# Eight-bank input transposes, the residual's affine step on VectorE, and a later table product in a one-core hybrid mLSTM / sparse-attention / MoE layer

## What is computed

```python
h = concat([meta_tokens, x])                # (528, 1024)
h = layer_norm(h, ln_in_g, ln_in_b)         # input norm: also the residual
p = h @ w_in                                # all projections
...                                         # mLSTM branch, sparse attention branch
ckv = rms_norm(c_kv, kv_norm_g)
logits += rel_bias[bucket(distance)]        # table of 32 buckets x 8 heads
h = layer_norm(ALPHA * h + y @ w_out, ...)  # the residual h is used here
h = layer_norm(ALPHA * h + moe(h), ...)     # 16 experts, two of them per token
```

## Time and profile before

| | us |
|---|---|
| median of 3 runs | 841.85 |
| lowest, highest | 839.75, 842.48 |
| the profiled execution's own time | 842.93 |
| its span in the trace | 840.8 |
| TensorE busy in the span | 747.8 (89%) |
| VectorE busy | 590.2 (70%) |
| ScalarE busy | 428.3 (51%) |
| GpSimd busy | 103.1 (12%) |

### The profile page before, as it was taken

How to read it: one execution, slowest core, us unless ns; L and a number is a source line. 1 busy time by engine, 2 the same in 40 slices (tenths; PEclk the granted TensorE clock), 3 DMA queues, 4 the chain that set the end, 5 groups by cost and what they waited for, 6 DMA issues and landing times.

```text
span 840.8 us, 10786 instructions
## 1 busy us (share of the span) xinstructions
PE 747.8 (89%) x3980; PEld 604.7 (72%) x3982; DVE 590.2 (70%) x794; ACT 428.3 (51%) x498; POOL 103.1 (12%) x118
## 2 busy tenths in 40 slices
PE   3399999999899999999999859999999999999920
PEld 1296799897467677787888756788888888888710
DVE  4906999796236544443565778898988989988828
ACT  4433333434642544481222133778778787878712
POOL 4540000000001000000000202111112121112012
PEclk9999999999999899999999958999999999999975
DMA  8645231320050111143238863999999999995243
GB/s 198 201 127 195 85 99 53 101 87 14 0 202 3 50 52 51 51 178 123 101 95 317 323 225 104 358 397 385 397 398 400 396 396 391 398 395 215 64 191 131
DMA packets 102540, 167.09 MB, mean 199 GB/s; under 512 B 18848, under 2 KB 39584, under 8 KB 102504
## 3 DMA queue, kind: packets, MB, share of 16 engines
q1 hardware_dynamic: 95024, 145.53, 48.8%
q0 software_dynamic: 4752, 13.11, 4.0%
q10 hardware_dynamic: 2728, 7.95, 2.4%
HBM read 156.07 MB, written 17.42 MB: 206 GB/s over the span
## 4 chain that ended last, share of the span: by engine, by line
PE 81%; DVE 9%; ACT 3%; issue 3%; DMA 2%; SPq 1%; POOL 0%; POOLq 0%; DVEq 0%; ACTq 0%
PE low L1032 15%; PE low L1033 15%; PE low L1034 15%; PE wide L1032 7%; PE wide L1034 7%; PE wide L1033 7%; PE wide L1407 2%; PE low L1202 1%; PE low L1302 1%; PE wide L1187 1%; PE low L1264 1%; PE low L1359 1%; PE wide L1235 1%; SPq L397 1%; PE wide L1420 1%
## 5 line engine op out<-in xcount | busy, mean ns | idle before, releaser
L1791 DVE TENSOR_TENSOR m_lo<-m_raw,m_hi 128x2048 fp32r<-128x2048 f32 x95 | 214.9, 2289 | 28.8 <-ACT m_hi L911 28.1
L911 ACT ACTIVATE m_hi<-m_raw 128x2048 fp32r<-128x2048 f32 x95 | 179.8, 1918 | 23.8 <-PE low L1034 23.5
L1032 PE MATMUL low<-m_hi,xe_hi 128*128 128x512 f32 x256 | 103.0, 402 | 2.7 <-DVE xe_lo L1856 1.8
L1032 PE MATMUL low<-hT_hi,w_hi 128*128 128x512 f32 (+1 forms) x240 | 95.7, 399 | 10.6 <-issue 10.6
L1034 PE MATMUL low<-m_hi,xe_lo 128*128 128x512 f32 x256 | 100.0, 391 | 0.0
L1033 PE MATMUL low<-m_lo,xe_hi 128*128 128x512 f32 x256 | 99.7, 389 | 0.0
L1509 DVE TENSOR_TENSOR w_lo<-raw,w_hi 128x2048 fp32r<-128x2048 f32 x28 | 64.1, 2290 | 45.7 <-ACT w_hi L654 45.5
L1033 PE MATMUL low<-hT_lo,w_hi 128*128 128x512 f32 (+1 forms) x240 | 93.7, 390 | 0.0
L1034 PE MATMUL low<-hT_hi,w_lo 128*128 128x512 f32 (+1 forms) x240 | 93.0, 388 | 0.0
L654 ACT ACTIVATE w_hi<-raw 128x2048 fp32r<-128x2048 f32 x28 | 53.5, 1909 | 18.1 <-PE wide L1034 8.3
L1032 PEld LDWEIGHTS low<-hT_hi,w_hi 128*128 128x128 f32 x240 | 47.2, 197 | 20.4 <-issue 11.1
(11 more groups left out here) (348 smaller groups left out, 1438.4 us busy)
## 6 DMA issues: line engine op xcount, KB each, us to landing
m_raw<-in_w_gate SPq DMA_DIRECT2D x32, 1024.0 KB, 8.2
m_raw<-in_w_up SPq DMA_DIRECT2D x32, 1024.0 KB, 8.0
m_raw<-in_w_down SPq DMA_DIRECT2D x31, 1024.0 KB, 9.2
raw<-in_w_in SPq DMA_DIRECT2D x19, 1024.0 KB, 5.1
raw<-in_w_out SPq DMA_DIRECT2D x4, 1024.0 KB, 5.0
table_dram<-table_row ACTq DMA_DIRECT2D x1, 2624.0 KB
strips<-table_dram SPq DMA_DIRECT2D x8, 264.0 KB, 4.1
xn<-in_x SPq DMA_DIRECT2D x4, 512.0 KB, 5.6
```

The costliest lines, as they stand in the source:

```text
L911: nc.scalar.activation(m_hi[n % MS][:, :], (m_spare if is_last(n, j) else m_raw[slot])[:, :], ACT.Copy).then_inc(q["m_hi_ready"], 1)
L1032: nc.tensor.matmul(outp, lh, rh, start=first, stop=False)
L1791: v.tensor_tensor(m_lo[n % MS][:, :], (m_spare if is_last(n, j) else m_raw[n % MR])[:, :], m_hi[n % MS][:, :].bitcast(F32), ALU.subtract). ...
```

## The change

Five edits, all at the start of the program:

1. Each row tile's eight transposes are made as soon as the tile is normalised, into eight banks (block c into bank (4 + c) mod 8). The second pass of transposes with its wait on `lo_x` is gone. The meta transposes go to bank 4 and wait for `lo_x` at 1.
2. The residual's scale and bias move from GpSimd to VectorE, behind `w_lo` of unit 1.
3. ScalarE makes `w_hi` of unit 0 after block 1 of `hT_hi` and no longer before block 0.
4. The table product moves on TensorE from the front to just before the transposes L1119. `ftab` and its store move on ScalarE behind the second `qidxT`. Their two loads go behind `gbc` and `bbc`, which go ahead of the other late loads.
5. The squares go to `score` in place of `md`, so ScalarE's wait on `h_stored` moves down to the store of `table_dram`. GpSimd makes the two triangular masks between the powers of tiles 0, 1 and 2.

```diff
 @block.sync
-            sp.dma_start(relb[:, :], a["rel_bias"]).then_inc(q["table_in"], 16)
-            sp.dma_start(oneh[:, :], onehot).then_inc(q["table_in"], 16)
...
             load(1)
+            sp.dma_start(gbc[:, :], bcast_rows(a["ln_in_g"], D)).then_inc(q["load_late"], 16)
+            sp.dma_start(bbc[:, :], bcast_rows(a["ln_in_b"], D)).then_inc(q["load_late"], 16)
+            sp.dma_start(relb[:, :], a["rel_bias"]).then_inc(q["table_in"], 16)
+            sp.dma_start(oneh[:, :], onehot).then_inc(q["table_in"], 16)
             for i in range(CONV):
...
-            sp.dma_start(gbc[:, :], bcast_rows(a["ln_in_g"], D)).then_inc(q["load_late"], 16)
-            sp.dma_start(bbc[:, :], bcast_rows(a["ln_in_b"], D)).then_inc(q["load_late"], 16)
 @block.gpsimd
...
                 pool.wait_ge(q["rstd_ready"], i + 1)
+                if i == 0:
+                    step(nc.gpsimd.memset(tri_qs[:, :], 0.0))
...
+                elif i == 1:
+                    step(nc.gpsimd.memset(tri_st[:, :], 0.0))
...
-            pool.wait_ge(q["load_late"], 16 * 10)
-            pool.wait_ge(q["xt_done"], KC)
-            for i in range(TT):
-                pool.wait_ge(q["xn_ready"], i + 1)
-                step(nc.gpsimd.tensor_tensor(xn[:, i, :], xn[:, i, :], gbc[:, :], ALU.mult))
-                nc.gpsimd.tensor_tensor(xn[:, i, :], xn[:, i, :], bbc[:, :], ALU.add).then_inc(q["h_ready"], 1)
-                pool.wait_ge(q["h_ready"], i + 1)
 @block.scalar
-            act.wait_ge(q["table_done"], 1)
-            nc.scalar.activation(ftab[:, :], wide[0][0:AH, 0:FX], ACT.Copy).then_inc(q["table_out"], 1)
-            act.wait_ge(q["table_out"], 1)
-            act.dma_start(table_row, ftab[:, :]).then_inc(q["table_put"], 16)
...
-            split_hi(0)
             act.wait_ge(q["load_consts"], 16 * 2)
             for c in range(KC):
+                if c == 2:
+                    split_hi(0)
                 act.wait_ge(q["xt_done"], c + 1)
...
-            act.wait_ge(q["h_stored"], 16 * TT)
             for i in range(TT + 1):
...
-                square = nc.scalar.activation(md[0:n, 0:R], src, ACT.Square, accum_out=css[0:n, i:i + 1])
+                square = nc.scalar.activation(score[0:n, 0:R], src, ACT.Square, accum_out=css[0:n, i:i + 1])
...
-            act.wait_ge(q["h_stored"], 16 * TT)
             evac(B_QI, qidxT[:, 0, :])
             evac(B_QI + 1, qidxT[:, 1, :])
+            act.wait_ge(q["table_done"], 1)
+            nc.scalar.activation(ftab[:, :], wide[0][0:AH, 0:FX], ACT.Copy).then_inc(q["table_out"], 1)
+            act.wait_ge(q["table_out"], 1)
+            act.dma_start(table_row, ftab[:, :]).then_inc(q["table_put"], 16)
             split_hi(3)
+            act.wait_ge(q["h_stored"], 16 * TT)
 @block.tensor
...
-                for c in range(4):
-                    mm = nc.tensor.transpose(bank[4 + c][:, i * P:(i + 1) * P], xn[:, i, c * P:(c + 1) * P], ident[:, :])
+                for c in range(KC):
+                    mm = nc.tensor.transpose(bank[(4 + c) % 8][:, i * P:(i + 1) * P], xn[:, i, c * P:(c + 1) * P], ident[:, :])
...
-            for c in range(4, KC):
-                pe.wait_ge(q["lo_x"], c - 3)
-                for i in range(TT):
-                    mm = nc.tensor.transpose(bank[c][:, i * P:(i + 1) * P], xn[:, i, c * P:(c + 1) * P], ident[:, :])
-                mm.then_inc(q["xt_done"], 1)
             pe.wait_ge(q["xm_ready"], 1)
+            pe.wait_ge(q["lo_x"], 1)
 @block.vector
...
             split_lo(1)
+            dve.wait_ge(q["load_late"], 16 * 10)
+            for i in range(TT):
+                step(v.tensor_tensor(xn[:, i, :], xn[:, i, :], gbc[:, :], ALU.mult))
+                v.tensor_tensor(xn[:, i, :], xn[:, i, :], bbc[:, :], ALU.add).then_inc(q["h_ready"], 1)
```

More of the change, by code:

```diff
@@ L522, in _ @@
                 pool.wait_ge(q["rstd_ready"], i + 1)
+                if i == 0:
+                    step(nc.gpsimd.memset(tri_qs[:, :], 0.0))
+                    step(nc.gpsimd.affine_select(out=tri_qs[:, :], in_=tri_qs[:, :], compare_op=ALU.is_ge, fill=NOT_CAUSAL,
+                                                 base=0, pattern=[[-1, P]], channel_multiplier=1))
+                elif i == 1:
+                    step(nc.gpsimd.memset(tri_st[:, :], 0.0))
+                    step(nc.gpsimd.affine_select(out=tri_st[:, :], in_=tri_st[:, :], compare_op=ALU.is_ge, fill=NEG_MASK,
+                                                 base=0, pattern=[[1, P]], channel_multiplier=-1))
             for h in range(MH):
                 step(nc.gpsimd.tensor_copy(sel_row[64:68, h, :], ident[64:68, 64 + h:65 + h].to_broadcast([MH, P])))
[L526 to L531, removed]
             step(nc.gpsimd.memset(mask[:, 0:P], 0.0))
@@ L663, in _ @@
                 nc.scalar.activation(xn[:, i, :], xn[:, i, :], ACT.Identity, bias=shift0[:, i:i + 1], scale=rstd[:, i:i + 1]).then_inc(q["xn_ready"], 1)
-            split_hi(0)
             act.wait_ge(q["load_consts"], 16 * 2)
             for c in range(KC):
+                if c == 2:
+                    split_hi(0)
                 act.wait_ge(q["xt_done"], c + 1)
                 if c % 2:
-                    nc.scalar.activation(hT_hi[:, c, META:T], bank[4 + c % 4][:, :], ACT.Identity,
+                    nc.scalar.activation(hT_hi[:, c, META:T], bank[(4 + c) % 8][:, :], ACT.Identity,
                                          bias=lnb[:, c:c + 1], scale=lng[:, c:c + 1]).then_inc(q["hi_x"], 1)
@@ L675, in _ @@
                     act.wait_ge(q["lo_x"], c - 1)
-                step(nc.scalar.activation(tmpT[:, c % 2, :], bank[4 + c % 4][:, :], ACT.Identity,
+                step(nc.scalar.activation(tmpT[:, c % 2, :], bank[(4 + c) % 8][:, :], ACT.Identity,
                                           bias=lnb[:, c:c + 1], scale=lng[:, c:c + 1]))
@@ L1060, in by_token @@
                 return mm
[L1062 to L1065, removed]
             pe.wait_ge(q["const_done"], 1)
@@ L1068, in _ @@
                 pe.wait_ge(q["xn_ready"], i + 1)
-                for c in range(4):
-                    mm = nc.tensor.transpose(bank[4 + c][:, i * P:(i + 1) * P], xn[:, i, c * P:(c + 1) * P], ident[:, :])
+                for c in range(KC):
+                    mm = nc.tensor.transpose(bank[(4 + c) % 8][:, i * P:(i + 1) * P], xn[:, i, c * P:(c + 1) * P], ident[:, :])
                     if i == TT - 1:
                         mm.then_inc(q["xt_done"], 1)
-            for c in range(4, KC):
-                pe.wait_ge(q["lo_x"], c - 3)
-                for i in range(TT):
-                    mm = nc.tensor.transpose(bank[c][:, i * P:(i + 1) * P], xn[:, i, c * P:(c + 1) * P], ident[:, :])
-                mm.then_inc(q["xt_done"], 1)
             pe.wait_ge(q["xm_ready"], 1)
+            pe.wait_ge(q["lo_x"], 1)
             for c in range(KC):
-                mm = nc.tensor.transpose(bank[2][:, c * META:(c + 1) * META], xm[0:META, c * P:(c + 1) * P], ident[0:META, 0:META])
+                mm = nc.tensor.transpose(bank[4][:, c * META:(c + 1) * META], xm[0:META, c * P:(c + 1) * P], ident[0:META, 0:META])
             mm.then_inc(q["xt_done"], 1)
@@ L1116, in _ @@
             by_channel(take(B_QI + 1)[:, :], 1, P, META, T).then_inc(q["block_done"], 1)
+            pe.wait_ge(q["table_in"], 32)
+            nc.tensor.matmul(wide[0][0:AH, 0:512], relb[:, :], oneh[:, 0:512], start=True, stop=True)
+            nc.tensor.matmul(wide[0][0:AH, 512:FX], relb[:, :], oneh[:, 512:FX], start=True, stop=True).then_inc(q["table_done"], 1)
             pe.wait_ge(q["c_ready"], TT + 1)
@@ L1122, in _ @@
             pe.wait_ge(q["block_out"], B_QI + 2)
+            pe.wait_ge(q["table_out"], 1)
             index_scores(0)
@@ L1538, in _ @@
                         dve.wait_ge(q["lo_x"], c - 1)
-                    step(v.tensor_scalar(tmpT[:, 1, :], bank[4 + c % 4][:, :], lng[:, c:c + 1], lnb[:, c:c + 1], ALU.mult, ALU.add))
+                    step(v.tensor_scalar(tmpT[:, 1, :], bank[(4 + c) % 8][:, :], lng[:, c:c + 1], lnb[:, c:c + 1], ALU.mult, ALU.add))
                 v.tensor_tensor(hT_lo[:, c, META:T], tmpT[:, c % 2, :], hT_hi[:, c, META:T].bitcast(F32), ALU.subtract).then_inc(q["lo_x"], 1)
@@ L1542, in _ @@
             wide_c = lambda t: t[:, :].rearrange("p (c o) -> p c o", o=1).to_broadcast([P, KC, META])
-            step(v.tensor_tensor(tmpM[:, :, :], bank[2][:, 0:KC * META].rearrange("p (c x) -> p c x", c=KC), wide_c(lng), ALU.mult))
+            step(v.tensor_tensor(tmpM[:, :, :], bank[4][:, 0:KC * META].rearrange("p (c x) -> p c x", c=KC), wide_c(lng), ALU.mult))
             v.tensor_tensor(tmpM[:, :, :], tmpM[:, :, :], wide_c(lnb), ALU.add).then_inc(q["affine_m"], 1)
```

## The result

| | before | changed |
|---|---|---|
| median, us | 842.16 (4 runs) | 832.32 (4 runs) |
| lowest, highest | 839.75, 845.07 | 829.46, 833.48 |
| profiled execution, and its span | 842.93, 840.8 | 833.48, 831.6 |
| first projection starts at | 40.30 | 30.02 |
| small transposes behind `c_tok` start at | 68.45 | 57.67 |

The ratio is 0.988, with a 95% interval of 0.9857 to 0.9902: 9.8 us faster. A second measurement of the same kernel, beside 17 runs of the kernel before, gave 831.52 against 843.11 (ratio 0.9863, 0.9842 to 0.9884).

The account below looks back on a forecast made before the run. TensorE, 81% of the chain, was taken as the bound, with 10.6 us waiting for `hT_lo` before the first projection. Gains 6.9 + 3.1 + 1.5 = 11.5 us from 842.4 gave 831 us, range 828.5 to 836.

Parts of the forecast that it names:

- GpSimd off the residual: VectorE before the first projection: operations stretched beside GpSimd's residual work return to unstretched length, 6.9 us (bounds 0 and 6.9).
- The earlier start: ScalarE's first blocks and weight split ahead of the first projection: `hT_lo` of block 2 comes 3.1 us earlier.
- The 0.9 us from SP's queue: Head of SP's queue: without two table loads, x, statistics and normalised tiles come 0.9 us earlier (bounds 0.3 and 0.9).
- The transposes' removal from between the blocks costs nothing: TensorE before the first projection: dropping the second pass of transposes from between the blocks costs 0.
- The rise of the clock: TensorE's 32 unbroken transposes: clock rises at about 15, block 0 complete at 16.0; without it 0.6 us less gain.
- GpSimd's small operations beside the first `hT_lo`: Near the first `hT_lo`: GpSimd's small copies and mask operations contend with VectorE; the sum could lose some tenths.
- The residual on VectorE, cost 0: VectorE behind `w_lo` of unit 1: eight operations of 1.14 us, 9.1 us, covered by 10 us of slack before `css`.
- The table product, cost 0: TensorE's 2.0 us wait for `c_tok`: product of about 1.3 us fits, cost 0; 0.6 at the slow clock level.
- The clock stays up, 1.5 us: TensorE behind the small transposes: only 0.7 us stay idle, so the clock holds; 1.5 us gained (bounds 0 and 1.5).
- late weights: Rival, ScalarE's split amid the blocks: first weights land late, each us past 18.1 costs one; 834 at 21; chance 0.10.
- the late loads: Rival, VectorE's residual waits for all ten late loads with `css` behind: slower, 847 at landing 60; chance 0.03.
- clock falls all the same: Rival, behind L1119: the small table product may not count as work; 10.0 us gained, 832.4; chance 0.26.

## Why the prediction was right

The forecast was 831 us in a range of 828.5 to 836; measured were 832.3 and, again, 831.5. As a gain, 11.5 us were forecast, 9.8 measured, and 11.6 in the repeat. The mechanism of the largest term is shown; that the sum came out so well is in part luck, as the steps show:

- **GpSimd off the residual, 6.9 us.** Shown, as a mechanism and in size: 6.8 us of stretch left when the residual moved alone, and the stretch came back, larger, when GpSimd was released early. What the step didn't see is that it is one of two ways to the same end. It took GpSimd's start at 29.79 as given and didn't ask what sets it. In the two runs with GpSimd's work in its old place, at 30.17 and 29.81, it is the landing of the late loads, `kvg` the last. In the profile before the row names a transpose of the meta columns, but GpSimd waits for the ones ahead of it, which were over at 28.8; that the loads set it there too is inferred. With VectorE's chain some 3 us earlier and unstretched, it is over 0.7 to 0.9 us before GpSimd may begin. So the two parts of the sum don't add freely. At the first projection the residual alone gives 8.2 us (1.4 of them the early weights of that execution), all the rest without it 10.9, both 10.3.
- **The earlier start, 3.1 us.** What is left of the 10.3 us beside 6.8 is 3.5, near the forecast, but the terms were others. 2.0 us are the order on ScalarE (shown). The other 1.4 or so is no effect of an edit as far as the runs show: with the split first and x loaded early the weights landed at 16.39, with SP's list of the kernel before at 16.45, and at 17.88 only in the profile before. The forecast counted from that late landing; that its 1.4 us stood in for terms that failed is luck. The 0.9 us from SP's queue became 1.3 at the first statistics and, in the two profiles of the change, 0 by block 0. "The transposes' removal from between the blocks costs nothing" failed by up to 0.6 us where the transposes speed up late: all 32 stand ahead of block 0. That freeing the banks earns nothing held. The 0.28 us per transpose was too long: that row was limited by the tiles' arrival, and in an unbroken run they take 0.21 to 0.23. The rise of the clock, for which I had counted 0.6 us, came late or not at all: the last group took 0.60 us in the repeat and 1.06 in the first profile. The two errors nearly cancelled, and block 0 came at the 16.0 that I took (15.86 and 16.01).
- **GpSimd's small operations beside the first `hT_lo`,** some tenths at most: such meetings occur and cost no more than that. In the first profile a mask operation of GpSimd took 0.56 us for 0.29 beside an `hT_lo` that kept its 0.69; in three other runs this first `hT_lo` took 0.73 to 0.82.
- **First projection at 30.3:** 30.02 and 30.17.
- **The residual on VectorE, cost 0:** held, at 1.22 us each for the 1.14 of the estimate, with 8.9 us of slack left.
- **The table product, cost 0:** held; 1.2 us inside the gap, ScalarE's part hidden.
- **The clock stays up, 1.5 us:** failed in the profile taken with the result, held in the repeat. Over all profiles the clock fell behind this place in 3 of 3 with 2.0 us idle, in 6 of 7 with 0.8 us idle, and in 0 of 3 with none. So the term of 1.5 us was mis-sized: it came in one profile of the changed kernel and not in the other. Whether the shorter gap makes the fall rarer at all isn't shown by 6 of 7 against 3 of 3. The reading that 0.7 idle us are "nearer to the 1.0 us row" compared lengths of gaps only.

The 1.3 us by which the result lies over the forecast is about this term; the repeat, whose profiled execution is without the fall, lies 0.5 us over it. That is a fit within the noise, not a proof: whether the clock fell in the executions that weren't profiled isn't known. The rivals: late weights didn't come (they were there at 17.9), the late loads landed in time, and the "clock falls all the same" case, 832.4, is what the first measurement looks like.

Open stays why the clock fell at 58 us in one profile of the changed kernel and not in the other, and why its low stretches at 200 and 518 us differ between executions; for the latter two no run was made.

## What to carry to other kernels

When an engine's operations are stretched beside another's, there are two cures: move the work, or see that the two never meet; ask what releases the other engine, since here a wait for loads it didn't need decided the whole gain. The second cure is free but hangs on 0.7 to 0.9 us between VectorE's last operation and a landing; the first one holds whatever lands when.

Price each edit of a bundle alone and all of them but one. Here the two large edits could both be spared; the order on ScalarE was worth 2.0 us at the first projection, and the table product's place 0.9 to 1.7 us of the time. The squares' new place and the masks were never tried alone.

A profile of the kernel before is one execution too: a landing that came 1.4 us later in it than in a run with the same loads went into the forecast as if every execution had it.

## What the runs showed of the hardware

- A VectorE operation with both inputs in SBUF waits out a GpSimd operation that reads SBUF: 128x512 pairs took 5.62 and 4.74 us for 1.50. Operations with one input in PSUM kept 0.80. The wait goes both ways: GpSimd's operation beside a `w_lo` of VectorE took 4.31 to 4.51 us for 2.34 to 2.41. The Trainium skill, SBUF — State Buffer, section Who interferes with whom, gives this rule, and the runs agree with it in all these rows.
- Behind a wait of TensorE of 0.8 us, with the table product just ahead of it, the granted clock fell to 0.50 for some 3 us in 6 of 7 profiles and not in the seventh, with the same program. Where TensorE had products all through, the table product's 32 rows among them, it did not fall in 3 of 3. The first profile of the changed kernel has two low stretches that the repeat lacks, at 58 and at 518 us, and its span is 3.2 us longer, more than some of the edits here were worth.
- The column of the granted clock can mislead near the start: it reads 1.00 from 40 to 45 in the earlier trace rows, where products of 264 columns start every 0.22 us, as they do at 0.50 in the changed kernel (30 to 34 us); behind the rise they start every 0.12.
- Fp32 transposes of 128x128 in an unbroken run start every 0.21 to 0.23 us at first and every 0.11 to 0.13 in the last groups of some executions; with the same instructions up to there the change came in the fifth group of four in one and in the seventh in another.
